# A hybrid decoder step on one core: in the recurrence, the r and k projections from seven half-size products, weight sums on GpSimd, squares on ScalarE

## The reference

```python
p_shift, q_mem, gate = jnp.split(h @ w_in, RWKV_SPLITS, axis=-1)
s = p_shift + (prev - p_shift) * mu
r, k, v, wl, al = jnp.split(s, SHIFT_SPLITS, axis=-1)
...
kk = (kf * k_k).reshape(hs)
kk = kk / jnp.maximum(jnp.sqrt(jnp.sum(kk * kk, axis=-1, keepdims=True)), 1e-12)
k_mod = (kf * (1.0 + (a - 1.0) * k_a)).reshape(hs)
y, wkv = wkv_recurrence(r_h, decay, k_mod, v_h, kk, a, wkv0)
mean = jnp.mean(y, axis=-1, keepdims=True)
var = jnp.mean(jnp.square(y - mean), axis=-1, keepdims=True)
yn = ((y - mean) * lax.rsqrt(var + GN_EPS)).reshape(b, t, TOK_WIDTH) * ln_w + ln_b
```

## Time and profile before

| | us |
|---|---|
| median of 3 runs (range) | 1728.71 (1726.29 to 1731.7) |
| the profiled execution's own time | 1735.68 |
| its span in the profile | 1734.0 |
| turns -1 to 9 (their first L1171 at 975.66, turn 10's at 1438.74) | 463.1 |
| TensorE busy, VectorE busy | 94%, 61% of the span |

### The profile page before, as it was taken

The page is one execution under the profiler, slowest core; times in us unless marked ns, Lnnn a source line. Parts: engine busy times, 40 slices in busy tenths (PEclk is TensorE's granted clock), DMA queues, the critical chain, the costliest instruction groups (busy, mean ns, idle before and its releaser), DMA issues.

```text
span 1734.0 us, 27840 instructions
## 1 busy us (share of the span) xinstructions
PE 1627.5 (94%) x9596; PEld 1289.5 (74%) x9596; DVE 1058.9 (61%) x4997; ACT 392.2 (23%) x978; POOL 161.4 (9%) x295
## 2 busy tenths in 40 slices
PE   7999998899999999979989999999999999899995
PEld 6677776677777777658967777777777777788895
DVE  4786556646464555528862477777777777340755
ACT  2131111101121121220120333333333333221011
POOL 1121212112112212220000000000000000020000
PEclk9999999999999999999989999999999999999998
DMA  9699999999999999994452233333333323374431
GB/s 387 224 343 396 419 406 391 373 393 420 419 408 419 405 416 416 353 365 196 146 237 74 83 100 102 101 101 101 101 101 101 101 77 116 108 272 170 146 146 51
DMA packets 101726, 419.95 MB, mean 242 GB/s; under 512 B 41797, under 2 KB 46289, under 8 KB 91985
## 3 DMA queue, kind: packets, MB, share of 16 engines
q0 software_dynamic: 41680, 218.91, 31.9%
q1 hardware_dynamic: 53256, 187.54, 28.5%
q10 hardware_dynamic: 6648, 11.73, 1.8%
HBM read 405.28 MB, written 12.85 MB: 241 GB/s over the span
## 4 chain that ended last, share of the span: by engine, by line
PE 76%; DVE 10%; ACT 5%; DMA 5%; issue 2%; POOLq 0%; POOL 0%; SPq 0%; ACTq 0%; DVEq 0%
PE psum L733 25%; PE psum L1160 10%; PE psum L801 10%; PE psum L783 6%; PE psum L1023 5%; DMA kvr<-in_cv 3%; PE psum L722 3%; PE psum L771 2%; PE psum L1207 2%; DMA kvr<-in_ck 1%; PE psum L1217 1%; PE psum L759 1%; PE psum L744 1%; ACT gT L1759 1%; PE psum L824 1%
## 5 line engine op out<-in xcount | busy, mean ns | idle before, releaser
L1921 DVE CUSTOM_DVE_ANT_0 kvr<-kvr,arena 128x128 f32<-128x128 f32 x1488 | 323.5, 286 | 111.5 <-DMA kvr<-in_ck 111.4
L733 PE MATMUL psum<-hT,wring 128*128 128x264 f32 x1536 | 364.3, 394 | 0.0
L733 PEld LDWEIGHTS psum<-hT,wring 128*128 128x128 f32 x1536 | 291.1, 193 | 67.7 <-issue 19.6
L1160 PE MATMUL psum<-hT,kvr 128*128 128x264 f32 x1152 | 284.4, 392 | 1.8 <-DVE hT L2249 1.8
L1160 PEld LDWEIGHTS psum<-hT,kvr 128*128 128x128 f32 x1152 | 214.2, 192 | 42.8 <-issue 8.9
L783 PE MATMUL psum<-hT,kvr 128*128 128x264 f32 x512 | 121.4, 393 | 0.0
L1921 DVE DVE_READ_ACCUMULATOR2_ANT arena<- 128x1 f32 x1488 | 121.3, 82 | 0.0
L783 PEld LDWEIGHTS psum<-hT,kvr 128*128 128x128 f32 x512 | 97.5, 194 | 16.9 <-issue 0.4
L667 POOL DMA_DIRECT2D kvr<-in_cv x128 | 68.0, 531 | 379.4 <-PE psum L1023 302.8
L1023 PE MATMUL psum<-kvr,arena 128*32 128x384 f32 x1024 | 97.6, 497 | 4.8 <-DMA kvr<-in_cv 4.8
L667 POOL DMA_DIRECT2D kvr<-in_ck x128 | 67.9, 530 | 216.7 <-issue 216.0
(11 more groups left out here) (433 smaller groups left out, 2322.6 us busy)
## 6 DMA issues: line engine op xcount, KB each, us to landing
kvr<-in_ck POOLq DMA_DIRECT2D x128, 768.0 KB, 11.9
kvr<-in_cv POOLq DMA_DIRECT2D x128, 768.0 KB, 11.2
kvr<-in_wrkv SPq DMA_DIRECT2D x12, 3072.0 KB, 13.4
kvr<-in_wo SPq DMA_DIRECT2D x14, 2048.0 KB, 8.2
wring<-in_wkv SPq DMA_DIRECT2D x12, 2048.0 KB, 11.9
wring<-in_wm SPq DMA_DIRECT2D x8, 2048.0 KB, 12.7
wring<-in_wg SPq DMA_DIRECT2D x8, 2048.0 KB, 12.2
kvr<-in_wg SPq DMA_DIRECT2D x8, 2048.0 KB, 8.5
```

The lines of the kernel that those rows point to most:

```text
L733: last = mm(psum[:, m % 2, 0:n], w[:, k, t * P:(t + 1) * P], rhs[:, k, 0:n], start=(k == 0), stop=(k == KT - 1))
L1160: last = mm(psum[:, m % 2, 0:T], w[:, k, t * P:(t + 1) * P], hT[:, k, :], start=(k == 0), stop=(k == KT - 1))
L1921: last = v_.tensor_tensor_reduce(page, page, qb[:, n % 2, h * P:(h + 1) * P], 1.0, 0.0, ALU.mult, ALU.add, S[:, n % 2, j * FH + h:j * FH + ...
```

## The change

For pairs 1 to 11 (turns -1 to 9) r and k come from seven products of 8 matmuls by 132 columns (Q1 to Q7), v stays as it was. The 56 + 16 matmuls are cut into 12 parts again (88 rows of `ROWS`, 7 or 8 a part; a v matmul counts as two). The sums of the four quarters of the input are made once, by GpSimd, in the place of `xT`, which is stored to memory before (`xkept`) and loaded again after the last pair. GpSimd also makes the four weight sums of each pair (128x1024 each), two of them in place in the weight buffer, each begun after a semaphore: the first after `prepared`, the second after `gn_ms`, the third after `tl_in` and the first three products, the fourth after `pair_done`. The conditions on `gn_ms` and `pair_done` hold from turn 1 on, that on `tl_in` from turn 0 on. VectorE joins the products in three places of a turn (`joined_pair`), ScalarE scales the joined r and k. Two squares (`df`, `gdf`) go from VectorE to ScalarE, and `centred` goes in front of `diagonals`, into `keys`. The kernel's core diff:

```diff
+            pool.wait_ge(sem("at_t"), 2 * MH + FH)
+            for u in range(1, RP):
+                m, at0, o = M_RKV + 3 * u, 4 * (FEW0 + u - 1), u - 2
+                a11, a12, a21, a22 = pair_weights(u % 2)
+                pool.wait_ge(sem(f"r_full{u % 2}"), 16 * (u // 2 + 1))
+                if u > 1:
+                    pool.wait_ge(sem("w_sum"), at0)
+                    pool.wait_ge(sem("p_done"), m - 1)
+                    pool.wait_ge(sem("prepared"), u - 1)
+                pt_(wsum1, fold(a21), fold(a22), ALU.add).then_inc(sem("w_sum"), 1)
+                pool.wait_ge(sem("w_sum"), at0 + 1)
+                if o >= 1:
+                    pool.wait_ge(sem("gn_ms"), o)
+                pt_(a21, a11, a21, ALU.subtract).then_inc(sem("w_sum"), 1)
+                pool.wait_ge(sem("p_done"), m + 1)
+                if o >= 0:
+                    pool.wait_ge(sem("tl_in"), o + 2)
+                pt_(wsum1, wsum1, fold(a11), ALU.subtract).then_inc(sem("w_sum"), 1)
+                pool.wait_ge(sem("w_sum"), at0 + 3)
+                if o >= 1:
+                    pool.wait_ge(sem("pair_done"), o)
+                pt_(fold(a12), fold(a12), wsum1, ALU.subtract).then_inc(sem("w_sum"), 1)
...
+                def pair_projected(t):
+                    m, sums = M_RKV + 3 * (o + 2), 2 * (FEW0 + o + 1)
+                    rest = 1 + TH
+                    if t == 0:
+                        return
+                    if t == 1:
+                        act.wait_ge(sem("om_out"), o + 3)
+                        if prepare:
+                            act.wait_ge(sem("mix"), o + 2)
+                        act.wait_ge(sem("y_out"), sums + 1)
+                        ac(pm[:, 1, :], pb[:, 1, 1:T + 1], ACT.Copy, scale=om[:, b, 1:2])
+                        ac(shout[:, 3 * (o + 2) + 1, :], pb[:, 1, NPR:T + 1], ACT.Copy)
+                        ac(pm[:, 0, 0:TH], pb[:, 0, 1:rest], ACT.Copy, scale=om[:, b, 0:1])
+                        return
+                    act.wait_ge(sem("p_done"), m + 3)
+                    act.wait_ge(sem("y_out"), sums + 2)
...
+                    act.wait_ge(sem("mix"), o + 2)
+                    ac(df, sx[:, 1, :], ACT.Square, scale=vec(K_K)).then_inc(sem("kk_sq"), 1)
+                if late:
+                    act.wait_ge(sem("gn_in"), 3 * (o - 1) + 2)
+                    ac(gdf, yT, ACT.Square).then_inc(sem("gn_in"), 1)
...
+                def joined_pair(part):
...
+                    dve.wait_ge(sem("p_done"), m + part + 1)
+                    if part == 0:
+                        ch.do(v_.tensor_copy(r1_, q(Q1)))
+                        v_.tensor_copy(k1_, q(Q5))
+                        tt(r0_, r1_, q(Q2), ALU.add).then_inc(sem("p_free"), 1)
+                    elif part == 1:
+                        ch.do(tt(r1_, r1_, q(Q6), ALU.add))
+                        ch.do(tt(k0_, r1_, q(Q7), ALU.add))
+                        ch.do(tt(r1_, r1_, k1_, ALU.add))
+                        ch.do(tt(k1_, k1_, k0_, ALU.add))
+                        ch.do(tt(k0_, k0_, q(Q4), ALU.add))
+                        dve.sem_inc(sem("p_free"), 1)
+                        dve.sem_inc(sem("y_out"), 1)
+                    else:
+                        tt(r1_, r1_, q(Q3), ALU.add).then_inc(sem("y_out"), 1)
...
                 def keys():
                     dve.wait_ge(sem("mix"), o + 2)
                     ch.do(ts(kkr, k, col(K_K), None, ALU.mult))
-                    tt(df, kkr, kkr, ALU.mult).then_inc(sem("kk_sq"), 1)
+                    if late:
+                        centred()
                     dve.wait_ge(sem("wa_out"), o + 2)
```

More of the change, by code:

```diff
@@ L458, in trunk_step, with fold, pair_weights, pair_bank @@
         u1, u2, u3, u4 = (arena[:, n * TH:(n + 1) * TH] for n in range(4))
+        psums = xT[:, :, :].rearrange("p k t -> p (k t)").rearrange("p (s k t) -> p s k t", s=4, k=KT // 2)
+        wsum1 = qT1[:, :, 0:2 * P].rearrange("p h (j n) -> p h j n", j=2)
+        UNITS1 = RP - 1
+        ROWS = [(q, k) for q in (Q2, Q1, Q5, Q4, Q7, Q6, Q3) for k in range(KT // 2)]
+        ROWS += [(Q3 + 1, k // 2) for k in range(2 * KT)]
+        CUT = [len(ROWS) * n // 12 for n in range(13)]
+        def fold(x):
+            return x.rearrange("p (h j) n -> p h j n", j=2)
+        def pair_weights(b):
+            w = runit[:, b, :].rearrange("p (k n) -> p k n", k=KT)
+            lo, hi = w[:, 0:KT // 2, :], w[:, KT // 2:KT, :]
+            return lo[:, :, 0:P], hi[:, :, 0:P], lo[:, :, P:2 * P], hi[:, :, P:2 * P]
+        def pair_bank(o, q):
+            m = M_RKV + 3 * (o + 2) + (Q2, Q1, Q5, Q4, Q7, Q6, Q3).index(q) // 3
+            return psum[:, m % 2, (Q2, Q1, Q5, Q4, Q7, Q6, Q3).index(q) % 3 * TH:][:, 0:TH]
         def few_slot(i):
@@ L796, in few_products @@
                 if i >= 2:
-                    pe.wait_ge(sem("y_out"), 2 * (i - 1))
+                    pe.wait_ge(sem("y_out"), 2 * (i - 1) + 2 * UNITS1 * layer)
                 def product(q, w, x):
@@ L815, in few_products @@
                 product(Q7, s3, t3).then_inc(sem("few_y"), 1)
[L816 removed]
+                pe.wait_ge(sem("w_sum"), 4 * (i + UNITS1 * layer) + 4)
                 product(Q3, s4, b22).then_inc(sem("p_done"), 2)
@@ L1163, in project_part, with pair_part @@
                         last.then_inc(sem("p_done"), 1)
+                def pair_part(n):
+                    a11, a12, a21, a22 = pair_weights(b)
+                    t1, t2, t3, t4 = (psums[:, i, :, :] for i in range(4))
+                    b11, b21, b22 = hT[:, 0:KT // 2, 0:TH], hT[:, KT // 2:KT, 0:TH], hT[:, KT // 2:KT, TH:T]
+                    sums = 4 * (FEW0 + o + 1)
+                    m = M_RKV + 3 * (o + 2)
+                    for at in range(CUT[n], CUT[n + 1]):
+                        q, k = ROWS[at]
+                        if at in (0, 24, 48):
+                            pe.wait_ge(sem("p_free"), m + at // 24 + 1)
+                        if q > Q3:
+                            if at % 2 == 0:
+                                last = mm(psum[:, m % 2, TH:TH + T], w[:, k, 2 * P:3 * P], hT[:, k, :], start=(k == 0), stop=(k == KT - 1))
+                                if k == KT - 1:
+                                    last.then_inc(sem("p_done"), 1)
+                            continue
+                        if k == 0:
+                            if q == Q5:
+                                pe.wait_ge(sem("t_sum"), 8)
+                                pe.wait_ge(sem("w_sum"), sums + 1)
+                            if q == Q7:
+                                pe.wait_ge(sem("w_sum"), sums + 2)
+                            if q == Q6:
+                                pe.wait_ge(sem("w_sum"), sums + 3)
+                            if q == Q3:
+                                pe.wait_ge(sem("w_sum"), sums + 4)
+                        s = wsum1[:, k // 2, k % 2, :]
+                        lhs, rhs = {Q2: (a12, b21), Q1: (a11, b11), Q5: (s, t1), Q4: (a22, t4), Q7: (a21, t3), Q6: (s, t2),
+                                    Q3: (a12, b22)}[q]
+                        last = mm(pair_bank(o, q), s if q in (Q5, Q6) else lhs[:, k, :], rhs[:, k, :],
+                                  start=(k == 0), stop=(k == KT // 2 - 1))
+                        if at in (23, 47):
+                            last.then_inc(sem("p_done"), 1)
                 def lora():
@@ L1744, in turn_of @@
                 solution(0)
-                projected(1)
+                if not -2 < o < RP - 2:
+                    projected(1)
                 right_side(1)
@@ L2267, in turn_of @@
                 zt = x3(Z[:, 0, :])
+                def joined_pair(part):
+                    if not -2 < o < RP - 2:
+                        return
+                    m, lhs, rest = M_RKV + 3 * (o + 2), slice(1, 1 + TH), slice(1 + TH, 1 + T)
+                    r0_, r1_, k0_, k1_ = pb[:, 0, lhs], pb[:, 0, rest], pb[:, 1, lhs], pb[:, 1, rest]
+                    q = lambda n: pair_bank(o, n)
+                    dve.wait_ge(sem("p_done"), m + part + 1)
[13 more added lines that the diff above has]
+                        tt(r1_, r1_, q(Q3), ALU.add).then_inc(sem("y_out"), 1)
                 def level(n):
@@ L2380, in turn_of @@
                     diagonals()
-                if late:
+                if late and not prepare:
                     centred()
```

55 lines of the change are left out of this document (44 added, 11 removed).

## The result

The changed kernel takes **1743.92 us** in the median of 8 runs (1735.34 to 1750.44), against 1729.69 (1726.29 to 1733.4) for the kernel before: a ratio of 1.0077, 95% interval 1.0058 to 1.0096. It is slower, by 14.2 us between the medians (13 by the ratio), and lies above the range of the prediction. The profiled execution took 1750.44 us, its span 1748.8.

What follows compares the result with a forecast made beforehand. VectorE's chain paces a turn up to `turn(0)`, TensorE after it. -10.8 (turns 1 to 9) + 2.4 (turns -1 and 0) + 3 (GpSimd's sums) = -5.4 us; from the runs' median, 1728.71, that gives 1723.3. Range 1710 to 1738.

Steps and rivals of the forecast that it cites:

- Half products, -1.04 in TensorE's half: In the half of a turn that TensorE paces, eight parts with half products save 1.04 us; the first four count nothing.
- Squares and `centred`, -0.81: VectorE's chain to `tl_in` gets 0.81 us shorter a turn with two squares on ScalarE and `centred` moved into a wait.
- ScalarE's end of turn, +0.65: ScalarE's copies start 0.45 us later and grow, so table load, sigmoids and L2294 come 0.65 later in turns 1 to 9.
- Turns -1 and 0, +2.4 without the sums: VectorE's tail has no slack there, so joins and later ScalarE copies cost 2.4 us together, before any GpSimd disturbance.
- The prediction's own step from 2.95 to 5.2 us: In turn 0, the time from the tail's end to `keys` grows from 2.95 to 5.2 us, entered as +2.1.
- GpSimd's sums: Sums of 2.4 us each delay VectorE by 0 to 11.8 us over turns -1 to 9; 3 taken.
- VectorE is held for the whole of every sum it meets: Rival: GpSimd's sums exclude VectorE's two-SBUF-input operations, price 11.8, sum +3.4, 1732 us; chance 0.3.
- Slower: the weight sums are long: Rival: weight sums above some 3 us reach over `mix` and `normal_keys`; at 3 us each, 1746 us; chance 0.15.
- The four input sums run in turn -2, beside attention: nothing: GpSimd's four sums of the inputs, made during turn -2's attention, were taken to cost nothing.
- a sign of being wrong: A granted clock that falls in the longer waits of turns -1 and 0 would show the prediction wrong; no size given.

Runs made afterwards that it cites:

- e1: The changed kernel with each GpSimd sum cut to one element, signals and order kept: 1731.54 us, ratio 1.0001.
- e2: The changed kernel with GpSimd's first weight sum begun at VectorE's second join instead of at the end of the turn before: 1736.43 us, ratio 1.0037.
- e5: e2 with ScalarE's six masked-block copies and their waits put ahead of its copies of r and k: 1728.79 us, ratio 0.9987.
- e4: The kernel before with only the squares edit, both squares on ScalarE and the centring ahead of the diagonals: 1723.25 us, ratio 0.9953.
- e9: The changed kernel with the edits of e2 and e5, input sums on VectorE, and sums of turns -1 and 0 gated too: 1722.14 us, ratio 0.9945.
- e14: e9 with VectorE's second join ahead of the block inverse and the first weight sum begun at the inverse's end: 1723.18 us, ratio 0.995.
- e10: e4 (whole products) with ScalarE's masked blocks put ahead of its last copy of the turn: 1721.71 us, ratio 0.9947.

## Why the prediction was wrong, step by step

- *Half products, -1.04 in TensorE's half*: right. B is 28.25 before and 27.20 in e1, e2 and e5 where no DMA is late.
- *Squares and `centred`, -0.81*: right, -0.81 in e4 (14.38 to 13.57).
- *ScalarE's end of turn, +0.65*: the mechanism right, the size 0.96 (13.57 to 14.53). The third join ends 0.2 us ahead of the turn's start (1100.08, 1100.27 in e2), not 0.35, and ScalarE begins 0.1 behind it: its start is 0.72 later than before (0.45 forecast), its copies 0.39 longer, less the 0.17 of slack. Over nine turns 2.8 us more than forecast.
- *Turns -1 and 0, +2.4 without the sums*: e1 has 78.15 against 77.47, +0.7. Against e4, which has the squares, it is +2.4. How much of a half-clock stretch falls there differs (the granted clock is 0.96 in before and e1, 0.98 in e4), so a size is not to be had from one profile each. (The prediction's own step from 2.95 to 5.2 us gives 2.25, not 2.1.)
- *GpSimd's sums*: their length right (2.4 forecast, 2.366 mean), their price wrong. I put it between 0 and 11.8 and took 3. Turns 1 to 9 cost 4.7 (forecast 0 to 6.3) and turns -1 and 0 6.0 (0 to 5.5): 10.7, almost the far end. The reason I gave, that only one of four sums meets an operation with two SBUF inputs, failed twice: a sum costs its full remaining length wherever it meets one, and an operation with one SBUF input can be held too. In turns 1 to 9 it was mostly the copy of eight elements, which reads SBUF once; with most of its hold gone (e2) 3.4 of the 4.7 go. The rival "VectorE is held for the whole of every sum it meets" was the right one. "Slower: the weight sums are long" named the right direction for a wrong reason, since no sum takes 3 us.
- *"The four input sums run in turn -2, beside attention: nothing"*: **this step failed outright**, +4.0. I looked at what needs the sums, not at what VectorE does beside them. The same lock that I priced for turns -1 to 9 was left out here. The clock that falls behind such waits, which I had named as a sign of being wrong, had no term either (0.95 and 0.88 granted in turns -2 and -1; 1.00 and 0.91 before).
- *Not in the prediction*: VectorE's slack of 3.42 us at the turn's end had hidden late near blocks. I spent it on the joins and counted only their own 1.65 us. Turns 1 to 9 exceed nine times 42.63 by 1.9 us before, nine times 41.81 by 1.2 in e4, and nine times 41.73 by 4.4 in e1: 2.5 us more than before. Of e1's 4.4, 3.6 stand in stretch B of turns 2, 3, 6 and 7. Before's 1.9 are no late blocks but 3.4 us at 1.2 GHz in turn 4 (its stretch A is 16.28), so the lost slack costs 3.6 and the profile before happened to be 1.9 long.

In sum: -5.4 + 4.0 + 7.7 (10.7 instead of 3) + 2.8 + 2.5 - 1.7 (0.7 instead of 2.4) = +9.9, and the windows show +9.75 from turn -2 to turn 9 (4.0 + 6.7 - 0.95). The terms are read from these same windows, so this says that none is forgotten, not that each is exact. The spans differ by 14.8 and the medians by 14.2; of the 4.9 ahead and behind, the 2.2 behind go with the clock (above), the rest stays without a cause. The range failed with it: even the held-VectorE rival ended at 1732, since its far end lacked turn -2, ScalarE's full delay and the lost slack.

So the change is -8 (squares), +8 (half products by themselves, e1 against e4: -9.4 of matmuls, +8.6 at ScalarE's end of turn, +3.2 of lost slack, +2.4 in turns -1 and 0, and 3.5 left over, for which I have no cause; in the two profiles 5.9 lie outside these stretches, with 73 us at 1.2 GHz in all in e1 and 53 in e4) and +13 (sums). With the waits mended (e9, e14) the half products come to the time of whole products with the same squares (e10, e4). No arrangement tried beat those, and the squares alone are the version to keep. What is open: why the near blocks land later in turns 2, 3, 6 and 7 of the kernels with half products, and whether the joins' cost in turns -1 and 0 can be had lower.

## What to carry to other kernels

Work put on GpSimd is not free because GpSimd is idle: go through what VectorE runs beside each of its operations, in every stage, and, as far as this kernel's traces show, pay what is left of the operation's length wherever VectorE copies or scales inside SBUF or reads it twice, and TensorE's clock after the wait (turn -2: 2.1 us of waiting and 1.9 at 1.2 GHz); then tie the operation to a signal behind which VectorE reads PSUM, divides or waits. An engine's slack ahead of a join is what hides the spread of DMAs; whoever spends it pays the spread too. And a wait moved onto an engine's last copies delays everything that stands behind them in its queue: look there for small work that can go ahead of the wait (e5).
